# Modulation of block 2: PE's sums over partitions replaced by row sums on VectorE, and four single steps put in another place

## The reference

```python
def first_block(x, ...):              # no modulation in it
    x = pool_mixer_layer(x, ...)      # rmsnorm, w_in, causal means, w_group, w_out
    k, v = shared_kv(x, ...)          # rmsnorm, kv_w_a, kv_w_b, norms of the keys, rope
    return mla_layer(x, k, v, ...)    # 16 heads, softmax, gate, w_out

def second_block(x, c, w_mod, b_mod, ...):
    mod = silu(c) @ w_mod + b_mod     # (1, 2048) @ (2048, 12288)
    sh1, sc1, g1, sh2, sc2, g2 = split(mod, 6)
    h = rms_norm(x, norm_attn) * (1 + sc1) + sh1
    # window attention (16 heads) and attention over selected keys (16 heads)
    x = x + g1 * (concat(out_a, out_b) @ w_out)
    h = rms_norm(x, norm_ffn) * (1 + sc2) + sh2
    x = x + g2 * conv_ffn(h)          # w_up, causal convolution, w_down
    return rms_norm(x, norm_final)
```

## Time and profile before

| | us |
|---|---|
| median of 3 runs | 2115.6 |
| the runs | 2108.03, 2115.6, 2126.04 |
| the profiled execution's own time | 2109.15 |
| its span | 2107.3 |
| PE busy | 2077.6 (99%) |
| DVE busy | 1570.2 (75%) |
| ACT busy | 1025.7 (49%) |
| POOL busy | 15.4 (1%) |

### The profile page before, as it was taken

The page is one execution under the profiler, slowest core; times in us unless marked ns, Lnnn a source line. Parts: engine busy times, 40 slices in busy tenths (PEclk is TensorE's granted clock), DMA queues, the critical chain, the costliest instruction groups (busy, mean ns, idle before and its releaser), DMA issues.

```text
span 2107.3 us, 41652 instructions
## 1 busy us (share of the span) xinstructions
PE 2077.6 (99%) x17914; PEld 2047.4 (97%) x17914; DVE 1570.2 (75%) x2054; ACT 1025.7 (49%) x1331; POOL 15.4 (1%) x23
## 2 busy tenths in 40 slices
PE   7999999999999999999999999999999999999998
PEld 7999999999999999989999899999999999999998
DVE  7988688588587888697755687698765766766666
ACT  5443444344445466564457557454434444444443
POOL 1000000000000000000000000000000000000000
PEclk9999999999999999999899999999999999999999
DMA  7897898788675688578654664678866666666663
GB/s 248 279 345 277 278 320 293 239 299 321 213 266 170 203 295 276 184 257 289 213 164 116 175 183 128 204 268 287 290 185 190 190 200 192 186 204 192 197 192 121
DMA packets 248463, 480.94 MB, mean 228 GB/s; under 512 B 26315, under 2 KB 59703, under 8 KB 248279
## 3 DMA queue, kind: packets, MB, share of 16 engines
q1 hardware_dynamic: 247519, 478.06, 69.7%
q0 software_dynamic: 528, 0.15, 0.0%
q10 hardware_dynamic: 232, 0.06, 0.0%
HBM read 476.07 MB, written 8.44 MB: 230 GB/s over the span
## 4 chain that ended last, share of the span: by engine, by line
PE 94%; DVE 3%; issue 1%; DMA 1%; ACT 1%; SPq 0%; DVEq 0%; ACTq 0%
PE acc L1893 88%; PE side L1893 3%; PE sums L1893 2%; DVE mod_acc L1171 1%; PE sums L2167 1%; DMA mod_raw<-in_w_mod 1%; DVE w_lo L1183 0%; DMA x_tok<-in_x 0%; PE sums L1950 0%; DVE m_prob L1566 0%; ACT prob L1034 0%; ACT w_hi L629 0%; ACT prob L1045 0%; DVE h_lo L1591 0%; DVE kq L1543 0%
## 5 line engine op out<-in xcount | busy, mean ns | idle before, releaser
L1183 DVE TENSOR_TENSOR w_lo<-raw,w_hi 128x1024 fp32r<-128x1024 f32 x681 | 831.8, 1229 | 424.1 <-ACT w_hi L629 418.9
L629 ACT ACTIVATE w_hi<-raw 128x1024 fp32r<-128x1024 f32 x681 | 718.6, 1059 | 838.8 <-PE acc L1893 747.8
L1893 PE MATMUL acc<-h_hi,w_hi 128*128 128x256 f32 x3600 | 859.0, 280 | 11.0 <-issue 6.3
L1893 PE MATMUL acc<-h_lo,w_hi 128*128 128x256 f32 x3600 | 850.7, 278 | 0.0
L1893 PEld LDWEIGHTS acc<-h_hi,w_hi 128*128 128x128 f32 x3600 | 680.6, 189 | 22.1 <-issue 16.1
L1893 PEld LDWEIGHTS acc<-h_lo,w_hi 128*128 128x128 f32 x3600 | 680.7, 189 | 0.1
L1893 PE MATMUL acc<-h_hi,w_lo 128*128 128x256 f32 x3600 | 487.4, 278 | 0.0
L1893 PEld LDWEIGHTS acc<-h_hi,w_lo 128*128 128x128 f32 x3600 | 446.3, 189 | 0.0
L1171 DVE SCALAR_TENSOR_TENSOR mod_acc<-mod_raw,silu_c,mod_acc 128x1024 f32<-128x1024 f32 x180 | 230.4, 1280 | 11.8 <-DMA mod_raw<-in_w_mod 11.6
L1893 PE MATMUL acc<-f_hi,w_hi 128*128 128x256 f32 x704 | 164.1, 276 | 0.0
L1893 PE MATMUL acc<-f_lo,w_hi 128*128 128x256 f32 x704 | 164.0, 276 | 0.0
(11 more groups left out here) (337 smaller groups left out, 2162.2 us busy)
## 6 DMA issues: line engine op xcount, KB each, us to landing
mod_raw<-in_w_mod SPq DMA_DIRECT2D x192, 512.0 KB, 6.1
raw<-in_w_up SPq DMA_DIRECT2D x176, 512.0 KB, 4.4
raw<-in_a_w_in SPq DMA_DIRECT2D x128, 512.0 KB, 4.9
raw<-in_w_down SPq DMA_DIRECT2D x88, 512.0 KB, 4.5
raw<-in_a_w_out SPq DMA_DIRECT2D x64, 512.0 KB, 5.1
raw<-in_w_in SPq DMA_DIRECT2D x52, 512.0 KB, 3.7
raw<-in_b_w_in SPq DMA_DIRECT2D x40, 512.0 KB, 5.1
raw<-in_a_w_group SPq DMA_DIRECT2D x32, 512.0 KB, 4.8
```

The costliest lines, as they stand in the source:

```text
L629: last = act.activation(w_hi[s][:, :], raw[s][:, :], ACT.Copy)
L1183: last = dve.tensor_tensor(w_lo[s][:, :], raw[s][:, :], f32(w_hi[s][:, :]), ALU.subtract)
L1893: return pe.matmul(o, lhsT, rhs, start=start, stop=stop, skip_group_check=True)
```

## The change

`w_mod` is handed to the kernel transposed, so that a tile has 128 outputs on its partitions and 1024 input channels in a row (4 KB in memory, as before). `silu(c)` is needed as a row on all partitions: `silu_row` (128x2048, in the place of `mod_acc`), loaded by a broadcast DMA of 1 MB and passed through ACT's Silu, twice, since the place is used by other data in between. DVE multiplies tile and row in place and gets the row's sum through `accum_out` in one column of `mod_part`. A vector then needs two additions of 128x16 on DVE (`take_mod`) and nothing of PE: `mod_sum` and `mod_columns` are gone. The pace of the last two vectors starts 20 slabs later and is steeper (0.67 tiles a slab, 0.50 before).

Four steps move. At the start ACT splits two slabs ahead of the first `h_hi` parts, not three. At the keys' norm PE's sums come at stage 6 of the `kv_w_a` gemm and its spread ahead of the rope gemm; root and reciprocal come two slabs earlier on ACT and DVE. In the last pair of heads `m_take_k` precedes `split_to(at + 5)`. In block 2 the latent spread moves from stage 37 to 40, the parts from 39 to 42, and the wait for `lat_norm` from the score at 38 to `index_turned` at 42.

```diff
-DUP_AT, IDX_PREP_AT, LAT_AT, TOP_AT = 10, 42, 34, 54
+DUP_AT, IDX_PREP_AT, LAT_AT, LAT_SPREAD_AT, TOP_AT = 10, 42, 34, 40, 54
-            (294, 128), (314, 148), (324, 148), (336, 160), (IN2_AT + 95, 160), (IN2_AT + 159, 192))
+            (294, 128), (314, 148), (324, 148), (336, 160), (IN2_AT + 115, 160), (IN2_AT + 163, 192))
...
                     if n == LATE_MODS:
                         sp.wait_ge(att[1]["mix_lo"], TILES)
+                        load_row()
...
                         if slabs.total() == RING:
+                            sp.wait_ge(x_squared, 4)
+                            load_row()
...
+            def silu_of_row():
+                rows_silu.step()
+                act.wait_ge(crow_in, 16 * rows_silu.value())
+                act.activation(silu_row[:, :], silu_row[:, :], ACT.Silu).then_inc(csilu_ready, 1)
...
-            split(3)
+            split(2)
             for j in range(KD // 2):
                 h_part(j, by_tile=True)
-                if j == 1 or j >= 3:
+                if j < 2 or j >= 3:
                     split(1)
             act.wait_ge(vec_ready, 1)
-            act.activation(silu_c[:, :], vec[:, V_C:V_C + KD], ACT.Silu).then_inc(csilu_ready, 1)
+            silu_of_row()
...
-                if s == LAT_AT + 5:
+                if s == LAT_SPREAD_AT + 2:
                     act.wait_ge(lat_norm, lats.value())
...
-                    if j < 2:
-                        if n:
-                            dve.wait_ge(mod_summed, n // MOD_TILES)
-                        ins = dve.tensor_scalar(o, x[:, :], silu_c[:, 0:1], None, ALU.mult)
-                    else:
-                        dve.wait_ge(mod_used, n - 1)
-                        ins = dve.scalar_tensor_tensor(o, x[:, :], silu_c[:, j // 2:j // 2 + 1], o, ALU.mult, ALU.add)
-                    ins.then_inc(mod_used, 1)
+                    if j == 0:
+                        dve.wait_ge(csilu_ready, 2 if n == LATE_MODS else 1)
+                        if v >= 2:
+                            dve.wait_ge(mod_ready, v)
+                    dve.scalar_tensor_tensor(x[:, :], x[:, :], 1.0, silu_row[:, half * 1024:(half + 1) * 1024], ALU.mult, ALU.mult,
+                                             accum_out=mod_part[:, v % 2, half, c:c + 1]).then_inc(mod_used, 1)
...
             def take_mod(v):
-                mods.step()
-                dve.wait_ge(mod_summed, mods.value())
+                dve.wait_ge(mod_used, (v + 1) * MOD_TILES)
                 m = flat(mod[:, bass.ds(v, 1), :])
-                dve.tensor_tensor(m, mod_cols, vec[:, bass.ds(v * KD + V_BMOD, KD)], ALU.add).then_inc(mod_ready, 1)
+                link(dve.tensor_tensor(m, mod_part[:, v % 2, 0, :], mod_part[:, v % 2, 1, :], ALU.add))
+                dve.tensor_tensor(m, m, vec[:, bass.ds(v * KD + V_BMOD, KD)], ALU.add).then_inc(mod_ready, 1)
...
+                if j == 3:
+                    sq_adds.step(3)
+                    squares.step(4)
+                    keys_inverse = norm_inverse()
                 if j < 6:
                     split(1)
-            sq_adds.step(3)
-            squares.step(4)
-            norm_root()
+            dve.wait_ge(inv_spread, keys_inverse)
...
                 if last:
                     m_low(0, 2)
+                    m_take_k(n % 2)
                 split_to(at + 5)
-                m_take_k(n % 2)
+                if not last:
+                    m_take_k(n % 2)
...
-            gemm(8, hk_hi, hk_lo, four, before=h_ready(8))
-            norm_sums([k_sq[0]], 3)
+            def key_norm(s):
+                h_ready(8)(s)
+                if s == 6:
+                    norm_sums([k_sq[0]], 3)
+
+            gemm(8, hk_hi, hk_lo, four, before=key_norm)
+            norm_spread()
             gemm(1, hk_hi, hk_lo, [(0, ROPE)], k=KD, n=ROPE)
-            norm_spread()
...
-                gates(stages(n), mod_columns(3, soft_read) if n == 5 else None)
+                gates(stages(n))
...
             norm_sums(tmp, 2)
-            mod_sum(norm_spread)
+            norm_spread()
...
-                    if ATT_SCORES[0][p] > LAT_AT + 3:
-                        pe.wait_ge(lat_norm, 3)
...
             def index_turned():
                 evicted(4)
-                pe.wait_ge(att[0]["max"], TILES)
+                pe.wait_ge(lat_norm, 3)
```

More of the change, by code:

```diff
@@ L223, in two_block_kernel @@
         gain2 = low("gain2", [P, KD])
-        silu_c = low("silu_c", [P, KD])
+        mod_part = low("mod_part", [P, 2, 2, KD])
         rel = low("rel", [3 * BUCKETS, 2 * HEADS])
@@ L233, in two_block_kernel @@
         warm = low("warm", [P, 1])
-        mod_acc = home(MOD_AT, W_AT)("mod_acc", [P, D])
+        silu_row = home(MOD_AT, W_AT)("silu_row", [P, D])
         ring = home(W_AT, MID)
@@ L252, in two_block_kernel @@
         rms_sum, lat_sum, rms_cols = sums[:, 0, 0:TOK], sums[:, 1, 0:TOK], sums[:, 0, 0:HALVES]
-        m_squares, mod_cols = side[:, 1, SC:SC + 8], side[:, 0, SC:SC + KD]
+        m_squares = side[:, 1, SC:SC + 8]
         acc_banks = [a[:, :, :].rearrange("p (b j) t -> p b (j t)", b=2) for a in acc]
@@ L724, in _ @@
                 for half in range(HALVES):
-                    o = flat(tmp[half][:, :, :]) if m < 2 else mod_acc[:, half * 1024:(half + 1) * 1024]
+                    o = flat(tmp[half][:, :, :]) if m < 2 else silu_row[:, half * 1024:(half + 1) * 1024]
                     last = act.activation(o[:, m % 2 * 512:(m % 2 + 1) * 512], x_tok[:, half, m * 512:(m + 1) * 512],
@@ L1162, in mod_tiles @@
                     n, j = mod_at.total(), mod_at.slot(MOD_TILES)
[L1163 removed]
+                    v, c, half = n // MOD_TILES, j // 2, j % 2
+                    x = mod_raw[n % MOD_RING]
                     dve.wait_ge(mod_landed[n % MOD_RING], mod_at.turn(MOD_RING, 1) * 16)
[L1165 to L1172 removed]
+                    if j == 0:
[4 more added lines that the diff above has]
+                                             accum_out=mod_part[:, v % 2, half, c:c + 1]).then_inc(mod_used, 1)
                     mod_at.step()
@@ L2011, in late_vectors @@
                     last.then_inc(vec_turned, 1)
-            mods = Count()
-            def mod_sum(between):
-                mods.step()
-                pe.wait_ge(mod_used, mods.value() * MOD_TILES)
-                if mods.total() > 1:
-                    pe.wait_ge(mod_ready, mods.value())
-                for n in range(KD):
-                    if n == 3:
-                        between()
-                    last = mm(mod_cols[:, n:n + 1], mod_acc[:, n * P:(n + 1) * P], ones[:, 0:1], start=n == 0, stop=n == KD - 1)
-                last.then_inc(mod_summed, 1)
-            def mod_columns(per=1, guard=None):
-                mods.step()
-                at = Count()
-                def between(s):
-                    for _ in range(per):
-                        n = at.total()
-                        if n == KD:
-                            return
-                        if n == 0:
-                            pe.wait_ge(mod_used, mods.value() * MOD_TILES)
-                            pe.wait_ge(mod_ready, mods.value())
-                            if guard:
-                                guard()
-                        last = mm(mod_cols[:, n:n + 1], mod_acc[:, n * P:(n + 1) * P], ones[:, 0:1], start=n == 0, stop=n == KD - 1)
-                        if n == KD - 1:
-                            last.then_inc(mod_summed, 1)
-                        at.step()
-                return between
             pools, ys = Count(), Count()
@@ L2058, in gated, with pool_out @@
                     pe.wait_ge(y_lo_ready, ys.value(s // 2 + 1))
-            def pool_out(g, sums_at=None):
+            def pool_out(g):
                 hi, lo = y_two[g == 2]
                 for m in range(4):
-                    gemm(4, hi, lo, four, before=gated, between=mod_columns() if m == sums_at else None)
+                    gemm(4, hi, lo, four, before=gated)
                 ys.step(2)
@@ L2359, in key_latent_spread @@
                 pe.wait_ge(lat_inv_ready, 1)
-                pe.wait_ge(att[0]["max"], sum(at < LAT_AT + 3 for at in ATT_SCORES[0]))
+                pe.wait_ge(att[0]["max"], TILES)
                 for half in range(HALVES):
@@ L2472, in _, with ff_up @@
             ffs = Count()
-            def ff_up(before=None, sums_at=None):
+            def ff_up(before=None):
                 for m in range(2):
-                    gemm(8, h_hi, h_lo, four, before=before, between=mod_columns() if m == sums_at else None)
+                    gemm(8, h_hi, h_lo, four, before=before)
             def ff_down(a):
@@ L2486, in _ @@
                 for a in range(2):
[L2487 removed]
+                    ff_up()
                     ff_down(a)
```

38 lines of the change are left out of this document (21 added, 17 removed).

## The result

The median of 20 runs is 2110.55 us (2090.07 to 2142.05); the kernel before, run beside it, 2116.08 us (2107.22 to 2126.04, 20 runs). The ratio of the runs is 0.9943, 95% interval 0.9917 to 0.9970: some 0.6% faster, where 28.5 us, 1.4%, were forecast. The ratio leaves out a kernel's runs that are over 1.5% above its fastest (here the three at 2126.74 and above), so it is not the quotient of the two medians, 0.9974. The median lies outside the range that was given, 2068 to 2105; the fastest eight runs lie inside it.

A forecast was written before the change was run, and what follows sets the result against it. PE's matmul stream was taken to bound the kernel (94% of the span). Terms of 15.4 + 3.6 + 4.3 + 1.0 + 1.7 + 3.0 - 0.5 gave 28.5 us, 2080.7 against the profiled execution; 2084 was named, range 2068 to 2105.

The forecast's parts named there:

- The beat: PE's matmul stream: one slab every 2.72 us, read from two neighbouring slabs' first w_lo matmuls.
- Keys' norm: PE's 1.77 us wait behind DVE's kq at 675.59 goes; 1.7 us gained, down to 0.
- Last pair: Last pair of heads: the early m_take_k only shifts DVE's next wait; -0.5 us, between -3 and +4.9.
- Columns in gemms, gates and the norm: Modulation columns leave PE: 15.4 us inside gemms, 3.6 in the gates, 4.3 in the norm before block 2.
- Latent: PE's 2.00 us wait behind c_norm at 1163.13, plus slow matmuls after it, goes; 3.0 us, down to 1.5.
- Start: Kernel's start: ACT's third-slab copy moves behind two h_hi parts, so PE begins earlier; 1.0 us, range -0.5 to 1.6.
- DVE's tile: 192 accumulating multiplications on DVE replace its multiply-adds; extra cost taken as 0 outside the pairs of heads.
- Rival 1: Only the columns go, 19.0 us; each resolved stall comes back as the wait behind it; chance 0.17.
- rival 3: DVE's accumulating multiply runs at half rate, 1.28 us more a tile, about 2221 us in all; chance 0.07.

The follow-up runs named there:

- e6: Changed kernel plus 16 unread columns at each of the four old places inside gemms (v = 0, 1, 2, 5); twelve runs, 2106.87 to 2116.34 us.
- e1: Changed kernel again, unaltered; twelve runs in levels from 2089.8 us to near 2132, the profiled run at 2118.69.
- e10: Changed kernel once more, unaltered, profiled for its levels; 2114.51 us.
- e11: Changed kernel with ACT's split and m_take_k put back, plus one unread column in each of the FFN's first four blocks; 2080.74 to 2084.50, two near 2103 us.
- e2: Changed kernel with ACT's split of the sixth slab back behind the last h parts at the keys' norm; 2083.19 to 2086.76 and 2127.34 us, ratio 0.9882.
- e3: Changed kernel with m_take_k behind split_to(at + 5) in the last pair again; ten runs, lowest 2086.41 us, ratio 0.9939.
- e7: Changed kernel with ACT's split and m_take_k put back, plus 15 unread single columns across first stage and FFN; 2085.18 to 2088.84 us, ratio 0.9877.
- e4: Changed kernel plus 16 unread columns in the first stage's second gemm and 16 in the FFN's; 2097.0 to 2122.7 us, one run at 4184.56.
- e13: Changed kernel with ACT's split and m_take_k put back, plus eight unread single columns across first stage and FFN; median 2085.24 us, ratio 0.9869.

## Why the prediction was wrong

- **The beat** is the step that put the median outside the range. "The stream's beat is one slab" was read as 2.72 us from two neighbouring slabs and taken for a constant. The profile before has the other value too (11 slabs of 2.83 from 568 us, 19 from 969, 13 from 1323), in stretches that the prediction never looked at; these are slow in every kernel, and show only that the beat has two values. The columns were priced at what they cost, 0.24 us each, and that price is right; what they were worth was not in the sum. By e6, those of v = 5 bounded a slow beat in the FFN to 70 slabs, 7.5 us. Those of v = 0, 1 and 2 stood every 60 to 70 slabs in the first stage; that they bounded it there is inferred from the times, since no profile of a kernel with them has a slow beat in that stretch. Without them a slow beat that begins at the FFN's pause lasts 260 slabs, 28 us (e1), one that begins at 1528 us 199 slabs, 21 us (e10), one in the first stage 188, 20 us (e11).
- **Keys' norm**, forecast 1.7 gained, measured 5.4 lost. "Late next would be the slab itself, which is loaded" looked at the load of the slab. It was the slab's place in the ring, for which ACT's copy waited 4.30 us with two `h` parts queued behind it. The description before the prediction puts the root behind the sixth slab on ACT as on DVE and names only root and reciprocal as moved; ACT's copy of the sixth slab, the line that costs the time, is named neither there nor in the prediction. e2 returns 6 to 7 us by that one line.
- **Last pair**, forecast -0.5, measured -2.9. The mechanism was right ("to let one wait earlier only shifts the next"), the size was off, though inside its bounds of -3 to +4.9: the idle moved to where the slow matmuls after it end the pair (e3), and a longer wait for a tile's load came with it.
- **Columns in gemms, gates and the norm**, 15.4, 3.6 and 4.3 forecast, 15.2, 3.6 and 3.4 to 4.8 measured. **Latent**, 3.0 against 3.8. **Start**: PE's first matmul came at 17.63 for 18.68, and 0.75 of that was left at 186 us, for the 1.0. **DVE's tile** +0.02 us, for 0.
- The sum by measured terms is 15.2 + 3.6 + 3.4 + 0.8 - 5.4 + 3.8 - 2.9 = 18.5, which is 2090.7 from the profiled execution before; lowest to lowest gave 17.2. Of the 11 us missing to 28.5, 7 are the keys' norm and 2.4 the last pair. These alone would have left the time at 2090.7 by the profiled execution and 2097.1 by the median before, inside the range; the upper levels, with 12 of 20 runs, took the median out of it, and the three profiles of such runs of this kernel (the one above, e1, e10) have the slow beat in the FFN.
- **Rival 1** (each resolved stall comes back as the wait behind it) came near the lowest level, 17 for its 19, but partly by luck: the latent and the norm did gain, while two places lost more than they had. The half rate of rival 3 is refuted: 1218 ns, and 1.8 us was the mark.

What stays open: what the slow beat is, and why one column ends it. The granted clock is 1.00 in both, and neither idle time nor loads distinguish them; a pause and a 0.17 us wait can both bring it, neither always, and it also ended with no column near, twice at a gemm's first matmuls (e7, e11). Whether it is the column or any small break in the stream that turns it is therefore open. So is why three stretches are slow in every profile, the one from about 545 us even through 16 columns; the beat turns fast behind it at a gemm's border without a column. That e4's upper levels come from waits like e10's (75 slabs from 338 us for 2108, some 205 from 1530 for 2120) fits their distances, but no profile caught one. The runs at 2126 to 2142 were not caught either; 20 + 28 or 20 + 21 above the lowest level would give 2138 and 2131.

## What to carry to other kernels

Work that seems to be pure overhead in a stream of matmuls can hold the stream's pace: when it goes, measure the step of the matmuls in every long stretch, ahead of the change and behind it, and not the busy share, which is 98 to 99% at either pace. If a kernel's runs stand in levels, divide the distances by the loss per slab; the count of slabs that comes out points at the stretch, and a profile of such a run confirms it. When a step is moved on an in-order queue, ask for each wait behind which it now stands whether it waits for data or for a place that the late engine must free.

## What was not expected of the hardware

- A matmul of 128x256 here has two steps, 113 and 118 ns (24 to a slab of 2.72 or 2.83 us), both at a granted clock of 1.00. It keeps one for up to 261 slabs.
- It turned slow behind a wait of 0.17 us (e10). In both profiles where a slow stretch of the FFN met one column, 0.24 us, it was fast behind it (e11, e13); sixteen columns did not turn the stretch at 568 us. Of the two kernels without a run on an upper level, e7 and e13, the latter pays 1.9 us for eight single columns and took 2083.69 to 2087.49 in five runs, 1.3% less than the kernel before.
- DVE's multiply with an accumulator took 1218 + 82 ns for 128x1024, the multiply-add without one 1279.
